# Where the on-chip buffers of a two-block transformer kernel begin: 128 bytes past a multiple of 256

## The reference

```python
x = x + 0.5 * swiglu(rms_norm(x, ffn1_norm), w_gate, w_up, w_down)   # d_ff 2816, second block 2752
x = x + mixer(rms_norm(x, mix_norm))
x = x + 0.5 * swiglu(rms_norm(x, ffn2_norm), w_gate, w_up, w_down)
```

## The kernel before

| tile | starts at | by 256 |
|---|---|---|
| X, Xh, Xl | 16512, 32896, 49280 | 128 |
| raw, wh, wl (three each) | 65664 to 98432 | 128 |
| par (small constants, 1527 columns) | 102528 | 128 |
| ones, identR, maskR | 108704 on | 160 |
| rb, sq, acc, diag | 110368 on | 32 |
| Hh, Hl | 124832, 169888 | 160 |
| ft (three) | 214944 on | 160 |
| a_RB, a_QT, a_KT, a_Vh, a_Vl, a_P (stage 2) | 124832 on | 160 |
| c_Yh, c_Yl (stage 5) | 124832, 141216 | 160 |
| g_RB, g_KT, g_Vh, g_Vl, g_ABh, g_ABl, g_P (stage 8) | 124832 on | 160 |

## Time and profile before

### The profile page before, as it was taken

The page is one execution under the profiler, slowest core; times in us unless marked ns, Lnnn a source line. Parts: engine busy times, 40 slices in busy tenths (PEclk is TensorE's granted clock), DMA queues, the critical chain, the costliest instruction groups (busy, mean ns, idle before and its releaser), DMA issues.

```text
span 2809.6 us, 31389 instructions
## 1 busy us (share of the span) xinstructions
PE 2766.3 (98%) x12580; PEld 2261.5 (80%) x12580; DVE 1331.8 (47%) x1895; ACT 908.2 (32%) x1286; POOL 130.3 (5%) x130
## 2 busy tenths in 40 slices
PE   8999999999999999999999999999999999999998
PEld 6888878888888888888888888888877877788776
DVE  5444358654443444434654444344443557544432
ACT  4222226542322223222233232223222346432221
POOL 0000005300000000000000000000000114000000
PEclk9999999999999999999999999999999999999999
DMA  4332232033323333333333333333322320233322
GB/s 152 99 98 91 91 86 77 24 89 103 95 92 96 96 98 90 101 96 96 98 90 98 98 90 98 92 95 91 105 85 89 92 81 23 61 103 100 90 84 70
DMA packets 282704, 253.30 MB, mean 90 GB/s; under 512 B 8384, under 2 KB 278848, under 8 KB 282560
## 3 DMA queue, kind: packets, MB, share of 16 engines
q1 hardware_dynamic: 282560, 251.30, 29.9%
HBM read 249.17 MB, written 2.10 MB: 89 GB/s over the span
## 4 chain that ended last, share of the span: by engine, by line
PE 82%; issue 13%; DVE 3%; ACT 2%; DMA 0%; SPq 0%; POOLq 0%; POOL 0%; DVEq 0%
PE bank L380 27%; PE bank L381 27%; PE bank L382 27%; PE bank L469 1%; DVE a_mx L1235 0%; PE bank L433 0%; PE bank L422 0%; DMA raw<-in_ffn_w_gate 0%; DVE wl L1126 0%; ACT Xh L804 0%; DVE a_nb L1142 0%; ACT wh L773 0%; DVE a_KT L1138 0%; ACT a_P L857 0%; DVE X L1135 0%
## 5 line engine op out<-in xcount | busy, mean ns | idle before, releaser
L1126 DVE TENSOR_TENSOR wl<-raw,wh 128x1024 fp32r<-128x1024 f32 (+6 forms) x498 | 573.9, 1166 | 976.2 <-ACT wh L773 975.3
L380 PE MATMUL bank<-Xh,wl 128*128 128x512 f32 x2544 | 997.6, 392 | 12.9 <-DVE wl L1126 10.6
L382 PE MATMUL bank<-Xh,wh 128*128 128x512 f32 x2544 | 992.0, 390 | 0.0
L381 PE MATMUL bank<-Xl,wh 128*128 128x512 f32 x2544 | 991.5, 390 | 0.0
L773 ACT ACTIVATE wh<-raw 128x1024 fp32r<-128x1024 f32 (+6 forms) x498 | 494.9, 1009 | 1001.3 <-PE bank L382 994.9
L380 PEld LDWEIGHTS bank<-Xh,wl 128*128 128x128 f32 x2544 | 476.3, 187 | 117.0 <-issue 12.6
L381 PEld LDWEIGHTS bank<-Xl,wh 128*128 128x128 f32 x2544 | 476.4, 187 | 102.9 <-issue 1.9
L382 PEld LDWEIGHTS bank<-Xh,wh 128*128 128x128 f32 x2544 | 476.1, 187 | 103.0
L380 PE MATMUL bank<-Hh,wl 128*128 128x512 f32 x1056 | 419.0, 397 | 0.0
L382 PE MATMUL bank<-Hh,wh 128*128 128x512 f32 x1056 | 417.0, 395 | 0.0
L381 PE MATMUL bank<-Hl,wh 128*128 128x512 f32 x1056 | 417.0, 395 | 0.0
(11 more groups left out here) (264 smaller groups left out, 1583.5 us busy)
## 6 DMA issues: line engine op xcount, KB each, us to landing
raw<-in_ffn_w_gate SPq DMA_DIRECT2D x128, 512.0 KB, 3.8
raw<-in_ffn_w_up SPq DMA_DIRECT2D x128, 512.0 KB, 3.9
raw<-in_ffn_w_down SPq DMA_DIRECT2D x114, 512.0 KB, 3.5
raw<-in_c_w_in SPq DMA_DIRECT2D x24, 512.0 KB, 3.7
raw<-in_w_in SPq DMA_DIRECT2D x10, 512.0 KB, 3.8
raw<-in_a_w_in SPq DMA_DIRECT2D x8, 512.0 KB, 3.8
raw<-in_a_w_out SPq DMA_DIRECT2D x8, 512.0 KB, 3.5
raw<-in_c_w_out SPq DMA_DIRECT2D x8, 512.0 KB, 3.5
```

What stands on the lines that cost most here:

```text
L380: e.matmul(o, ll, rh, start=start, stop=False)
L381: e.matmul(o, lh, rl, start=False, stop=False)
L382: i = e.matmul(o, lh, rh, start=False, stop=stop)
L1126: e.tensor_tensor(lo, src, hi.bitcast(F), ALU.subtract).then_inc(wlo.up(("w", n)), 1)
```

## The change

Four edits. The constants inside `par` that are 64 columns or wider begin at a multiple of 64 columns, so `par` has 1600 columns in place of 1527, and the gaps are filled with zeros. `sb` puts a tile of 512 bytes or more at the next address that is 128 past a multiple of 256, smaller ones at the next multiple of 32 as before. The scratch at the bottom of SBUF is set to 1024 bytes in place of 16384. No instruction of any engine is added, dropped or moved; one transfer, that of `par`, is 73 columns wider.

```diff
@@ the constants' columns
+    _at = -(-_at // 64) * 64 if _n >= 64 else _at
     COLS[_name] = (_at, _at + _n)
     _at += _n
@@ build: sb
-            at = -(-place[0] // 32) * 32
-            place[0] = at + 4 * int(np.prod(shape[1:]))
+            size = 4 * int(np.prod(shape[1:]))
+            at = -(-(place[0] - 128) // 256) * 256 + 128 if size >= 512 else -(-place[0] // 32) * 32
+            place[0] = at + size
             return nc.alloc_sbuf_tensor_at(name, shape, dt, offset=at)
@@ kernel
-    par = np.empty((128, NCOLS), np.float32)
+    par = np.zeros((128, NCOLS), np.float32)
...
-    nc = _bacc.Bacc("TRN2", target_bir_lowering=False, num_devices=1)
+    nc = _bacc.Bacc("TRN2", target_bir_lowering=False, num_devices=1, dynamic_dma_scratch_size=1024)
```

## The result

The changed kernel takes 2786.86 us (median of 4 runs, 2785.77 to 2789.61) against 2809.77 us (median of 4). The ratio is 0.9918, 95% interval 0.9901 to 0.9935: 0.8% faster. The forecast was 2787 us.

The account below looks back on a forecast made before the run. TensorE bounds the kernel: matmul count times the step between starts. Gains of 20.8, 1.3, 0.6 and 0.3 us sum to 23.0 us, other terms 0, giving 2786.7 from the 2809.68 us median, forecast 2787 us, range 2781 to 2800.

Parts of the forecast that it names:

- H: Feed-forward down product: 3120 matmuls over Hh and Hl, brought from 160 to 128, each save 6.67 ns, 20.8 us.
- c_Y: 512-column matmuls over c_Yh and c_Yl, 3 x 64, gain 6.67 ns each from the move to 128: 1.3 us.
- g_AB: Fourier mixer's sequence transform: 3 x 32 matmuls with g_ABh or g_ABl stationary gain 6.67 ns each, 0.6 us.
- a_RB: 512-column matmuls with an a_RB operand, 3 x 16, gain 6.67 ns each from the move to 128: 0.3 us.
- the term that the prediction took as 0 with 3.8 us to either side: First attention, granted clock at 0.96: a shifted program may move the dips, 3.8 us less to 3.8 us more.
- The lower base: X, Xh, Xl, raw, wh, wl and par move down 15360 bytes with the smaller scratch: taken as 0.
- `par`: Start of the program: its transfer grows from 1527 to 1600 columns, costing between 0 and 0.4 us, taken as 0.
- The 64-row matmuls: Last feed-forward's last H tile and second attention's scores: gain at most 1.0 us, taken as 0.
- Something else that goes with H: Rival: the pace belongs to H's place in SBUF or reuse, TensorE gains nothing, 2809.7 us; chance 0.12.
- Only part comes back: Rival: 128 modulo 256 is not enough, streams settle at 230.4 ns, 10 us won, 2799.7 us; chance 0.06.
- Xh loses its step: Rival: the shift slows gate and up products to 233.3 ns, +50 us, H gains nothing, 2860 us; chance 0.04.
- The rule of 16-byte cachelines: Counter-rule for SBUF rows: 128 and 160 cross the same 128 lines, change worth nothing, 2809.7 us.

Follow-up runs that it names:

- H alone: Kernel before the change, with Hh and Hl moved from 160 to 128 past a multiple of 256: 2790.21 us against 2810.76 us, ratio 0.9928.
- All at 0: Changed kernel with large tiles at 0 instead of 128 past a multiple of 256: 2787.84 us, ratio 0.9918.
- all at 160: Changed kernel with every large tile at 160 instead of 128 past a multiple of 256: 2789.69 us, ratio 0.9922.
- the lower base alone: Kernel before the change with the smaller scratch only, every tile 15360 bytes lower, remainders by 256 kept: 2810.62 us, ratio 1.0.

## Why the prediction was right, point by point

- **The bound.** Right. TensorE's step set the time, and a shorter step shortened it by as much: splits, transfers and waits followed.
- **The sum.** 23.0 us were forecast from two medians; 22.9 us were measured (2809.77 - 2786.86). By term, from the start times of both traces: H 20.6 us (forecast 20.8), c_Y 1.3 us (1.3), g_AB 0.6 us (0.6), a_RB 0.3 us (0.3). The experiment on H alone gives 20.6 us for that term by itself.
- **The profiled executions** differ by more, 2811.45 - 2785.77 = 25.7 us. That is 2.8 us more than the medians. Of this, 1.6 us are the first wait, 9.9 us in the earlier trace rows and 8.3 us now. The change has no part in it: with H alone moved, where nothing of the start differs from the kernel before, that wait is 8.4 us. The first attention before holds two stretches of 3.4 us at half of full speed (the 1.2 GHz level), the one after a single one, from 475.2 us on; in the 10 us ahead of the first two TensorE was busy for 8.1 and 8.8 us, at the full clock. One such stretch less is worth up to 1.7 us, half its length. This is the term that the prediction took as 0 with 3.8 us to either side; that the two medians came within 0.1 us of the sum all the same is luck.

```profile
480.80:484.10 3.30, 3.30 (x11) 0.50 0.00 0
532.00:535.30 3.30, 3.30 (x9) 0.50 0.00 0
```

- **Costs taken as 0.** The lower base: nothing, by its own experiment. VectorE and ScalarE: 1331.2 and 906.7 us busy against 1331.8 and 908.2. `par`: 800.0 KB that landed after 8.2 us, against 8.6 in the earlier trace rows. The 64-row matmuls: the scores last 485 ns against 486 in the earlier trace rows, and the last H tile steps at 230.9 ns over Hl against 231.1, so the bound of 1.0 us kept for them was not used. For the scores there was nothing to win: g_KT and g_AB agreed already.
- **What I had wrong.** I read the earlier trace rows as "it is enough that one operand, either one, stands at 160", so that operands had to be at 128. The rows fit a distance just as well: in every slow stream the two operands stood 32 (or 128) bytes apart, and there was no 512-column stream of 128 rows in the trace with both at 160. The runs at 0 and at 160 decide for the distance. That the forecast did not suffer is luck: the change puts every operand at 128, which is right under either reading. All at 0 and all at 160, which the first reading calls slow, ran as fast.
- **The rivals.** "Something else that goes with H" fell with H alone and with the lower base alone; the earlier trace rows, on which I had leaned against it, behaves as it should, unchanged at 230.7 ns. "Only part comes back" and "Xh loses its step" fell with the windows after. The rule of 16-byte cachelines that the prediction quotes from the Trainium skill ("SBUF — State Buffer", section "Specifications (TRN2)"), by which 128 and 160 were the same, does not describe this effect: 226.7 ns against 233.3 ns. But starts 4 bytes past a multiple of 16 did cost, in two experiments (232.4 ns, and 234 to 240 ns).

## What to carry to other kernels

In a kernel that streams matmul after matmul, measure the step from start times or from the count in a window, not busy time or mean duration: a 3% difference stood between two streams that both read as 100% busy. For streams of 512 columns like these, place moving and stationary operands so that their starts agree modulo 256 (here within 16 bytes) and on a multiple of 16; which remainder it is did not matter for the three that were tried, 0, 128 and 160. A weight chunk whose row pitch is no multiple of 256 bytes breaks this by itself, as the 160-column one does.

## What the runs showed of the hardware that was not expected

- The price of a distance is about 6.5 ns for a matmul of 512 columns, and none was seen for 256. The earlier trace rows could not show this, since both operands stand at one place in each. But the stream of the earlier trace rows, 119.9 ns in the changed kernel, steps at 118.7 ns with the weights 128 bytes apart and at 116.5 to 116.9 ns in the kernel with the weights at 112, 144 and 240: apart is there, if anything, shorter.
- A mismatch of one stationary operand slows two matmuls, the one that uses it (by 7.3 ns) and the one during which it is loaded (by 5.7 ns).
- After a chunk 4 bytes apart, the stream takes about eight matmuls to return to its best step; after one 144 bytes apart, one.
- Two operands that both begin 4 bytes past a multiple of 16 step at 234 to 240 ns, slower than operands that are merely apart, and the moving one weighs more than the stationary one.
